# Depthwise convolution stage: seven taps instead of five on TensorE for the last strips, key copies on ScalarE, the last memory values cut into parts, column sums against 128 columns

## What is computed

```python
def conformer_conv(hn, w_pw1, b_pw1, w_dw, b_dw, ln_g, ln_b, w_pw2, b_pw2):
    u = hn @ w_pw1 + b_pw1
    a, g = jnp.split(u, 2, axis=-1)
    u = a * jax.nn.sigmoid(g)
    # depthwise, causal, 31 taps, one weight for each channel and tap
    u = lax.conv_general_dilated(u, kern, ..., padding=((CONV_WIDTH - 1, 0),), ...) + b_dw
    u = layernorm(u, ln_g, ln_b)
    u = jax.nn.silu(u)
    return u @ w_pw2 + b_pw2
...
mkv = rms_norm(mem, mem_norm_gain[l]) @ w_mem_kv[l]   # mem: 256 x 1024, to keys and values of 512 columns each
mk, mv = jnp.split(mkv.reshape(bsz, m, 2, XATTN_HEADS, XATTN_HEAD_DIM), 2, axis=2)
```

## Time and profile before

| | |
|---|---|
| runs | 2128.96, 2130.27, 2130.34 us; median 2130.27 |
| span of the profiled execution (first to last instruction) | 2127.2 us |
| profiled execution's own time | not listed apart; the median lies 3.1 us above the span |
| PE busy | 2098.9 us (99%) |
| DVE, ACT, POOL busy | 48%, 38%, 44% |
| mean granted TensorE clock | 0.997 of full |

### The profile page before, as it was taken

How to read it: one execution, slowest core, us unless ns; L and a number is a source line. 1 busy time by engine, 2 the same in 40 slices (tenths; PEclk the granted TensorE clock), 3 DMA queues, 4 the chain that set the end, 5 groups by cost and what they waited for, 6 DMA issues and landing times.

```text
span 2127.2 us, 26516 instructions
## 1 busy us (share of the span) xinstructions
PE 2098.9 (99%) x9908; PEld 1705.7 (80%) x9908; DVE 1014.4 (48%) x1580; ACT 805.4 (38%) x1243; POOL 936.1 (44%) x436
## 2 busy tenths in 40 slices
PE   9999999999999999999999999999999999999998
PEld 7777888888888866888888887878867888888887
DVE  7996623122356555532132355572454466254463
ACT  7766322122343157322222355352244343232232
POOL 5984544444444410444444442444443444444442
PEclk9999999999999999999999999999999999999999
DMA  5332432222222222232222221222211222322221
GB/s 193 133 115 79 145 113 82 96 100 97 99 81 99 100 90 90 80 117 81 100 97 99 99 91 49 104 82 98 98 60 60 99 90 97 106 84 100 97 99 60
DMA packets 33803, 205.31 MB, mean 97 GB/s; under 512 B 4512, under 2 KB 6688, under 8 KB 10672
## 3 DMA queue, kind: packets, MB, share of 16 engines
q1 hardware_dynamic: 33424, 199.87, 26.6%
q10 hardware_dynamic: 288, 4.19, 0.5%
HBM read 197.73 MB, written 6.32 MB: 96 GB/s over the span
## 4 chain that ended last, share of the span: by engine, by line
PE 60%; issue 23%; POOL 10%; DVE 5%; ACT 1%; DMA 0%; POOLq 0%; SPq 0%; DVEq 0%; ACTq 0%
PE gp L599 19%; PE gp L600 19%; PE gp L601 18%; POOL w_lo L493 9%; DVE ms L1554 3%; POOL pool_sum L516 1%; DMA h<-x_hbm 0%; PE gp L646 0%; PE gp L645 0%; PE gp L647 0%; PE ms L742 0%; PE ms L737 0%; PE gp L945 0%; PE gp L885 0%; DVE acc_sq L1551 0%
## 5 line engine op out<-in xcount | busy, mean ns | idle before, releaser
L493 POOL TENSOR_TENSOR w_lo<-raw,w_hi 128x1024 fp32r<-128x1024 f32 x350 | 848.0, 2426 | 1099.2 <-ACT w_hi L1071 1077.5
L599 PE MATMUL gp<-a_hi,w_hi 128*128 128x512 f32 (+1 forms) x1456 | 567.4, 390 | 1.8 <-DVE a_lo L1554 0.9
L601 PE MATMUL gp<-a_hi,w_lo 128*128 128x512 f32 (+1 forms) x1456 | 563.2, 387 | 0.0
L600 PE MATMUL gp<-a_lo,w_hi 128*128 128x512 f32 (+1 forms) x1456 | 563.1, 387 | 0.0
L1071 ACT ACTIVATE w_hi<-raw 128x1024 fp32r<-128x1024 f32 x349 | 365.5, 1051 | 505.9 <-PE gp L601 434.2
L600 PE MATMUL gp<-b_lo,w_hi 128*128 128x512 f32 (+1 forms) x1216 | 469.7, 386 | 0.0
L599 PE MATMUL gp<-b_hi,w_hi 128*128 128x512 f32 x1184 | 462.8, 391 | 0.0
L601 PE MATMUL gp<-b_hi,w_lo 128*128 128x512 f32 x1184 | 460.6, 389 | 0.0
L599 PEld LDWEIGHTS gp<-a_hi,w_hi 128*128 128x128 f32 x1456 | 273.5, 188 | 60.3 <-POOL w_lo L493 1.5
L600 PEld LDWEIGHTS gp<-a_lo,w_hi 128*128 128x128 f32 x1456 | 273.5, 188 | 56.5 <-issue 1.4
L601 PEld LDWEIGHTS gp<-a_hi,w_lo 128*128 128x128 f32 x1456 | 273.4, 188 | 55.5
(11 more groups left out here) (333 smaller groups left out, 1829.0 us busy)
## 6 DMA issues: line engine op xcount, KB each, us to landing
raw<-w_hbm SPq DMA_DIRECT2D x176, 1024.0 KB, 4.8
proj_scratch<-kT ACTq DMA_DIRECT2D x2, 2048.0 KB, 6.7
fbias<-negc_scratch SPq DMA_DIRECT2D x16, 256.0 KB, 3.4
h<-x_hbm SPq DMA_DIRECT2D x4, 512.0 KB, 7.5
u_pad<-proj_scratch SPq DMA_DIRECT2D x1, 2048.0 KB, 10.1
big<-proj_scratch SPq DMA_DIRECT2D x1, 2048.0 KB, 8.7
out_hbm<-h SPq DMA_DIRECT2D x8, 256.0 KB, 2.2
mem_raw<-mem_hbm SPq DMA_DIRECT2D x1, 1024.0 KB, 12.5
```

The source lines that it names most:

```text
L493: g.tensor_tensor(at(w_lo), src, f32(at(w_hi)), ALU.subtract).then_inc(w_lo_done, 1)
L599: pe.matmul(o, wh, xh, start=start, stop=False)
L600: pe.matmul(o, wh, xl, start=False, stop=False)
L601: return pe.matmul(o, wl, xh, start=False, stop=stop)
```

## The change

Six edits, all in this stage:

- `PE_TAPS` for pair 3 goes from 5 to 7. DVE does 19 instead of 21 taps for each strip, PE 7 instead of 5, and ACT writes 7 instead of 5 diagonals for each strip.
- The keys leave PSUM by ACT (`memory_keys`, four plain 128x256 copies between its tap products), no longer by DVE (`KEYS_TAP`). The row that scales them goes to `var` with the factor D in it, and POOL multiplies all four by it in one 128x1024 operation, behind slabs 28 and 29 and ahead of the pair sums.
- The second half of the values (slabs 26, 27) moves behind `mean(7)`. Its first tile runs right there, its second in parts of k between the column sums and around `spread`. ACT copies the first tile behind the squares.
- The column sums of the memory's mean square and of the layer norm's variance have 128 moving columns (`wide_columns`), where they had one; of the result one column of each tile is read. The matmul that cleared the bank and the `keep_busy` calls between the sums go, and of the last 12 `keep_busy` matmuls 6 stay.
- `first_blocks(pw2)` runs its third bank three steps behind (`lag=3`).
- ACT loads slab 30 behind the first silu and slab 31 behind the sixth, where both stood ahead of the silus.

```diff
-PE_TAPS = (0, 0, 0, 5)
+PE_TAPS = (0, 0, 0, 7)
...
         def pe_diag(s, n):
-            return T[:, 2 * s, n * P:n * P + P] if n < 4 else U[:, 1, s * P:s * P + P]
+            if n < 4:
+                return T[:, 2 * s, n * P:n * P + P]
+            place = (U[:, 1, 0:2 * P], U[:, 1, 2 * P:], acc_sq[:, 0:2 * P], acc_sq[:, 2 * P:])[n - 4]
+            return place[:, s * P:s * P + P]
...
 # GpSimd
             for s in range(2):
                 slab(Pos(pw2["slab"] + s))
+            g.wait_ge(mrow_done, 1)
+            keys = Pos(memkv["blk"])
+            for c in range(4):
+                g.wait_ge(evac[keys.slot(4, c)], keys.turns(4, c) + 1)
+            g.tensor_tensor(mk, mk, var[:, MEM:2 * MEM].unsqueeze(1).broadcast_to([P, 4, MEM]), ALU.mult).then_inc(keys_scaled, 1)
             for n, k in enumerate((0, 2, 4)):
                 g.wait_ge(csq_done, k + 2)
                 g.tensor_tensor(lsq[k], lsq[k], lsq[k + 1], ALU.add).then_inc(cpair_done, 1)
...
 # TensorE, memory_stat
-                        m = pe.matmul(ms[:, 1, t:t + 1], mem_sq[:, k, t * P:t * P + P], inv_d[:, 0:1], start=(k == 0), stop=(k == 7),
+                        m = pe.matmul(ms[:, 1, t * P:t * P + P], mem_sq[:, k, t * P:t * P + P], inv_d[:], start=(k == 0), stop=(k == 7),
...
+            def wide_columns(src, bank, first, last):
+                for t in range(QB):
+                    m = pe.matmul(bank[:, t * P:t * P + P], src[:, t * P:t * P + P], inv_d[:], start=(first and t == 0), stop=last,
+                                  skip_group_check=True)
+                return m
...
 # TensorE, behind the means of blocks 0 to 5
             slab_xs(Pos(memkv["slab"] + 4), Pos(memkv["blk"] + 4), M, 2)
-            slab_xs(Pos(memkv["slab"] + 6), Pos(memkv["blk"] + 6), M, 1)
             mean(6)
             mean(7).then_inc(mean_done, 1)
-            slab_xs(Pos(memkv["slab"] + 6), Pos(memkv["blk"] + 6), M, 2, first=1)
-            clear_columns(ms[:, 3])
+
+            def last_values(k0, k1, t=1):
+                slab_xs(Pos(memkv["slab"] + 6), Pos(memkv["blk"] + 6), M, t + 1, first=t, k0=k0, k1=k1)
+            last_values(0, 8, t=0)
             for n, k in enumerate((0, 2, 4)):
                 pe.wait_ge(cpair_done, n + 1)
-                columns(lsq[k], ms[:, 3], False, False)
-                keep_busy(1, ms[:, 2], A)
+                wide_columns(lsq[k], ms[:, 3], n == 0, False)
+                last_values(n, n + 1)
             pe.wait_ge(clast_done, 1)
-            columns(lsq[6], ms[:, 3], False, True).then_inc(cvar_done, 1)
-            keep_busy(5, ms[:, 2], A)
+            wide_columns(lsq[6], ms[:, 3], False, True).then_inc(cvar_done, 1)
+            last_values(3, 6)
             spread(1, ln_diag, ms[:, 1])
-            keep_busy(12, ms[:, 2], A)
-            first_blocks(pw2, B, ln["split"], n=3)
+            last_values(6, 8)
+            keep_busy(6, ms[:, 2], A)
+            first_blocks(pw2, B, ln["split"], n=3, lag=3)
...
 # ScalarE
-                act.activation(U[:, 0, 0:MEM], ms[:, 1, 0:MEM], ACT.Copy).then_inc(mrow_done, 1)
+                act.activation(var[:, MEM:2 * MEM], ms[:, 1, 0:MEM], ACT.Copy, scale=float(D)).then_inc(mrow_done, 1)
+
+            def memory_keys(a, b):
+                bp = Pos(memkv["blk"])
+                for c in range(a, b):
+                    wait_blk(act, bp, c)
+                    act.activation(mk[:, c, :], gp[:, bp.slot(4, c), 0:MEM], ACT.Copy).then_inc(evac[bp.slot(4, c)], 1)
...
             memory_values(0)
             next_w(Pos(28 - AHEAD))
             next_w(Pos(29 - AHEAD))
-            memory_values(1, (0,))
             act.wait_ge(proj_stored[1], 16)
             for k in range(8):
                 act.wait_ge(centred, k + 1)
                 act.activation(lsq[k], big[:, k], ACT.Square).then_inc(csq_done, 1)
-            next_w(Pos(30 - AHEAD))
+            memory_values(1, (0,))
             act.wait_ge(c_inv, 2)
             root_of(1, colv[:])
             diagonal(1, ln_diag)
-            next_w(Pos(31 - AHEAD))
...
                 act.activation(b_hi[:, k], U[:, k % 2], ACT.Copy).then_inc(hi_done, 1)
+                if k == 0:
+                    next_w(Pos(30 - AHEAD))
                 if k == 3:
                     memory_values(1, (1,))
+                if k == 5:
+                    next_w(Pos(31 - AHEAD))
...
 # VectorE
-            def memory_keys():
-                v.wait_ge(mrow_done, 1)
-                for c in range(4):
-                    bp = Pos(memkv["blk"])
-                    wait_blk(v, bp, c)
-                    stt(mk[:, c, :], gp[:, bp.slot(4, c), 0:MEM], float(D), U[:, 0, 0:MEM], ALU.mult, ALU.mult).then_inc(evac[bp.slot(4, c)], 1)
```

More of the change, by code:

```diff
@@ L45 @@
 OUT_TAP, U_TAP = ((7, 14), (3, 10), (6, 14)), ((17, 20), (8, 14), (10, 18))
-STAT_TAP, KEYS_TAP = 16, 11
+STAT_TAP = 16
 STATS = 8
@@ L296, in pe_diag, with tile_columns @@
         def pe_diag(s, n):
-            return T[:, 2 * s, n * P:n * P + P] if n < 4 else U[:, 1, s * P:s * P + P]
+            if n < 4:
+                return T[:, 2 * s, n * P:n * P + P]
+            place = (U[:, 1, 0:2 * P], U[:, 1, 2 * P:], acc_sq[:, 0:2 * P], acc_sq[:, 2 * P:])[n - 4]
+            return place[:, s * P:s * P + P]
+        def tile_columns(bank):
+            return bank.rearrange("p (t c) -> p t c", t=QB)[:, :, 0]
         def conv_end(i, s=1):
@@ L326, in build @@
             sem("msq_done"), sem("mstat_done"), sem("mvar_done"), sem("mrstd_done"), sem("mscaled"))
-        mturned, mdiag_done, mrow_done = sem("mturned"), sem("mdiag_done"), sem("mrow_done")
+        mturned, mdiag_done, mrow_done, keys_scaled = sem("mturned"), sem("mdiag_done"), sem("mrow_done"), sem("keys_scaled")
         meps_done = sem("meps_done")
@@ L618, in slab_ws, with slab_xs @@
                         hook()
-            def slab_xs(sp_, bp, x, tiles, first=0):
+            def slab_xs(sp_, bp, x, tiles, first=0, k0=0, k1=8):
                 pe.wait_ge(w_lo_done, sp_.at(2))
@@ L624, in slab_xs @@
                     b = free_bank(bp, t)
-                    for k in range(8):
+                    for k in range(k0, k1):
                         s, at = sp_.slot(RING, k // 4), k % 4 * 256
@@ L629, in slab_xs @@
                         m = three(gp[:, b, 0:256], xh, xl, wh, wl, k == 0, k == 7)
-                    m.then_inc(blk_done, 1)
+                    if k1 == 8:
+                        m.then_inc(blk_done, 1)
             def slabs_wide(at, x, group):
@@ L667, in gemm, with first_blocks @@
                             slab_ws(Pos(at["slab"] + s, RING, i), Pos(at["blk"] + s, RING, i), x)
-            def first_blocks(at, x, ready, n=2, hook=None, hook_k=8):
+            def first_blocks(at, x, ready, n=2, hook=None, hook_k=8, lag=0):
                 sp_, bp = Pos(at["slab"]), Pos(at["blk"])
                 banks = [free_bank(bp, c) for c in range(n)]
-                for k in range(8):
-                    if k == hook_k:
+                for j in range(8 + lag):
+                    if hook and j == hook_k:
                         hook()
-                    pe.wait_ge(lo_done, ready + k + 1)
+                    if j < 8:
+                        pe.wait_ge(lo_done, ready + j + 1)
                     for c in range(n):
+                        k = j - lag * (c == n - 1)
+                        if not 0 <= k < 8:
+                            continue
                         if k == 0:
@@ L1234, in _ @@
                           12: lambda: projected(1, 0, 4)})
-            tap_products(3, {4: [23], 5: [24], 6: [25], 7: [26], 9: [27]}, {1: lambda: projected(1, 4, 5), 3: lambda: projected(1, 5, 8)})
+            tap_products(3, {4: [23], 5: [24], 6: [25], 7: [26], 9: [27]}, {1: lambda: projected(1, 4, 5), 3: lambda: projected(1, 5, 8), 7: lambda: memory_keys(0, 2), 8: lambda: memory_keys(2, 3), 9: lambda: memory_keys(3, 4)})
             memory_values(0)
@@ L1707, in conv @@
                                 make_u(i + 1, b)
-                    if i == 3 and s == 1 and n == KEYS_TAP:
-                        memory_keys()
             v.wait_ge(row_done, 1)
@@ L1727, in _ @@
             v.wait_ge(cvar_done, 1)
-            inverse_column(1, ms[:, 3, 0:QB])
+            inverse_column(1, tile_columns(ms[:, 3]))
             diagonal(1, ln_diag)
```

2 lines of the change are left out of this document (1 added, 1 removed).

## The result

| | before | after |
|---|---|---|
| median of nine runs each | 2129.39 us (2128.57 to 2130.34) | 2134.45 us (2133.17 to 2136.01) |
| ratio | | 1.0023 [1.0015, 1.0032] |
| span of the profiled execution | 2127.2 | 2131.2 |
| that execution's own time | 2128.96 | 2133.17 |

The change costs 5.1 us between medians, 0.24%. The spans of the two profiled executions differ by 4.0 (their own times by 4.2). The median lies within the predicted range, and above the 4.3 us that the prediction took as the least that can be told from no change, so of its three outcomes it is "slower", which had 23%. The profiled execution is the fastest of the nine: its mean granted clock is 0.997, and the others show 0.995 to 0.997, the slowest the lowest.

The account below looks back on a forecast made before the run. PE, busy 99% of the span, was taken as the bound. Terms +0.7 at full clock, +1.1 first fall and +1.7 second fall sum to +3.5 us: 2130.27 becomes 2133.8, range 2129.0 to 2137.3.

Parts of the forecast that it names:

- DVE -4.0, and the wait ahead of `out_a(3, 0)`: DVE sheds four taps (2.7 us) and the keys (1.3); its wait for ACT's memory_row copy grows to 3.1.
- `mean(7)` and centring 3.0 earlier: PE, not DVE, ends last before the norm; mean(7) starts at 169.5 instead of 172.50, centring equally earlier.
- POOL: Later slabs 28 and 29 plus a 2.35 us multiply delay the pair sums; third pair ends 1.75 us later, at 181.2.
- Second wait and second fall: PE waits 5.4 us between the values' first tile and the first pair; half clock behind it costs 1.7.
- clock stays up: Rival: the clock doesn't fall at one or both PE waits; +0.7 to +2.4, 2131.0 to 2132.7 us; chance 24%.
- First wait and first fall: PE waits 3.7 us ahead of its first taps and the clock falls; 1.7 price, 0.6 hidden, +1.1 us.
- the clock stays up, 2.1 more: PE between 86 and 170 us: wide memory sums avoid the half clock, so PE gains 2.1 us more before its taps.
- the one-column fall: PE's drop to half clock near 88 us, during 32 one-column passes, costing 2.1 us; forecast to disappear.
- Up to `pw2`: Spread ends 0.3 us earlier at full clock, before the clock's prices; pw2's first matmul starts near 191.5 to 192.5.
- Slab 30 between the silus: Start of pw2: ACT's slab copy before the second silu stalls PE behind six matmuls, +1.0 us.
- slab 31 and the last copy are hidden: In pw2 from the fourth step on, three banks outlast ACT, so these later ACT copies cost nothing.
- POOL isn't in the way: Rival: the third pair comes with the squares, 3.0 us earlier; -4.0 in all, 2126.3 us; chance 10%.

Follow-up runs that it names:

- e1: The changed kernel with POOL's multiply of the keys moved behind the three pair sums; median 2131.77 us, +2.5 to before.
- e4: The changed kernel with PE_TAPS for pair 3 back to 5, the other five edits kept; median 2129.77 us, +0.5 to before.
- e3: The changed kernel with 22 more keep_busy matmuls in PE's long wait ahead of the first pair's column sum; median 2132.44 us, +3.2 to before.
- e2: The changed kernel with POOL's slabs 28 and 29 and the multiply of the keys all behind the pair sums; median 2132.00 us, +2.7 to before.
- f6: The changed kernel with ACT's copy of slab 30 ahead of the first silu and all values ahead of spread; median 2134.75 us, +5.0 to before.
- f7: The kernel of e2 with the norm's four diagonals all written by ACT, none by DVE; median 2128.09 us, -1.7 to before.
- f5: The kernel before with only the memory's mean square summed against 128 columns; median 2127.72 us, ratio 0.9993.
- g9: The kernel of f8 with 14 instead of 6 keep_busy matmuls ahead of first_blocks; median 2126.51 us, -3.5 to before.
- f8: The changed kernel with pair sums, slabs 28 to 31, then multiply; diagonals by ACT; slab 30 ahead of silus; 12 keep_busy ahead of taps; 2127.08 us.

## Why the prediction was right, and where it was off

*DVE -4.0, and the wait ahead of `out_a(3, 0)`.* Right: ACT's diagonals make the wait 0.76 longer, 3.11 us, forecast 3.1.

*`mean(7)` and centring 3.0 earlier.* Right: 3.3. DVE's last block is whole at 169.13 (forecast 169.2) and `mean(7)` starts at 169.19 (forecast 169.5): the two engines arrive together, where the prediction had PE last.

*POOL.* Right, and the heart of it. Slabs done at 174.66 (forecast 175.1), multiply 2.34 (2.35), third pair 181.13 (181.2). The last figure is partly luck: POOL was 0.4 early behind the multiply (177.00, forecast 177.4), and the first two pairs took 2.93 us instead of 2.52 while DVE's fourth pair ran beside them. e1 and e4 confirm both causes by taking each away: the multiply, and the two taps that hold back slabs 24 and 25.

*Second wait and second fall.* Right: 5.55 us (forecast 5.4), clock down from about 175 to 182. Price 1.7 forecast; e3 gives 1.5 in the traces and 1.9 between medians. The rule of the Trainium skill ("TensorE: Matmul & The Clock Gate", section "HAM oscillation") that was weighed there agrees with the trace at this wait. The rival "clock stays up" was thus not what happened at this wait. e3 shows what it would have given: 2132.4, inside its 2131.0 to 2132.7, but as a difference +3.2 against its +0.7 to +2.4, since the prediction's base was 0.9 high.

*First wait and first fall.* Off. Forecast were a 3.7-us wait ahead of the first taps, a fall there, and +1.1. The profiled execution shows 2.56 us and a clock of 1.00 behind it. The step that failed is "the clock stays up, 2.1 more", and with it the wait of 3.7: the one-column fall went as forecast, but the clock had by then fallen at 83, behind a wait that in before had left it up. PE so came later to its taps and waited less. In this execution the term is 0 in place of 1.1. In the profiles of e1, e2, f6 and f7 the wait is 3.9 us and the clock falls there, as forecast; the means then start 0.9 to 2.1 us later than in after. So both courses occur, and the code up to there doesn't settle which: in f5 it is that of before, and its clock fell at 83, that of before did not.

*Up to `pw2`.* Forecast +1.4 without the first fall; measured +1.34. The prediction's sign for this place, a first start at 191.5 to 192.5, was not met (191.05), by the missing first fall.

*Slab 30 between the silus.* The mis-sized term. Forecast 1.0; the last of the six matmuls from 191.05 starts at 192.27, the next would follow at about 192.5 and starts at 194.03, so the stall is 1.5. The 1.0 of ACT's copy is there, and on top DVE's second `b_lo` takes 0.93 us more while POOL works on the same slab, part of it in PE's shadow. All of `pw2` is 2.03 us longer. Matmul by matmul against before, 1.6 of it arise at this stall, 0.1 near 197 and 0.25 at 203.2, where DVE's last two `b_lo` take 2.23 us under POOL's slab 31 (200.21 to 202.61), 0.69 each elsewhere. So "slab 31 and the last copy are hidden" was not quite so. g9, without the first stall and with the clock up, still has 1.0 us more in `pw2` than before, of which 0.8 lies behind the same two `b_lo`:

```profile
194.07 4.44 DVE L1586 TENSOR_TENSOR b_lo<-U,b_hi 128x512 fp32r<-128x512 f32 x2 [1.03 <-ACT b_hi L1289]
```

There POOL's slab 31 and its multiply run from 192.74 to 197.95.

*Behind `pw2`.* Forecast nothing, and by the prediction's own words it is wrong "if anything moves behind 215 us". The profiled execution has +0.65 there, other kernels here +0.3 to +1.8 with the same code. In after it is 0.3 at 801 to 806 us and 0.35 at 1577, both times in a longer wait of PE for DVE (0.82 us for `nmax` at 1577, 0.45 before). Why DVE is later there is open. In e4, with +1.8, one part is a stretch of half clock at 770 to 775 us.

*The sum.* +3.5 was forecast, +4.0 is the profiled execution, +5.1 the medians. That +3.5 and +4.0 lie so close is in part luck: the first fall (1.1) was not in this execution, and the stall, slab 31 and the rest behind `pw2` brought 1.7 more than forecast. The forecast 2133.8 lies 0.6 from 2134.45 partly because its base, the median of three runs, was 0.9 above that of nine. That after's median lies 1.3 above its profiled run goes with the lower clock of the other runs. The first fall ahead of the taps, as in e1, e2, f6 and f7, would cost about that much; no such run of after is traced, so it stays a candidate.

*The rival "POOL isn't in the way"* gave 2126.3 as its time, 4.0 below before. It was wrong for this change. As a mechanism it is borne out in part: with the pair sums first alone (e2) the time is 2132.0, and only with the diagonals moved off DVE as well (f7, f8, g9) it is 2128.1 to 2126.5, 1.7 to 3.5 below before.

## What to carry to other kernels

An engine that ends earlier wins only as far as the next queue in line is free: before moving work to the bottleneck engine, follow what it now releases later (here ring slots for two weight slabs), and put nothing ahead of the operation that the chain waits for, however well its idle time seemed to cover it. A wait of TensorE can be paid twice, once as a wait and once as a lowered clock behind it (1.5 us in after, 0.6 in f8, nothing at 83 us), so fill waits you can't remove, and look at the rows behind each one. When a DVE operation takes longer than its shape takes elsewhere, look at what GpSimd was doing at that moment. Before two traces are compared, look whether the clock fell at the same places in both.
